# Sixteen chunks of the gate and up projections by seven half-size products where it were ten

## The chip, the cores and the metric

The kernel runs on one core of a Trainium2 chip. The metric is the device time of one execution in microseconds (us), the median of three runs. The engines are TensorE (PE, with its weight loads as PEld), VectorE (DVE), ScalarE (ACT), GpSimd (POOL) and SyncE (SP), which here only issues the loads of the weight stream.

## The reference

Two layers of a hybrid network on 512 tokens of width 1024 in float32. The change touches only the feed-forward part, which is computed twice with different weights (FFN1 and FFN2):

```
D_MODEL, SEQ, D_FF = 1024, 512, 2816

def _swiglu(x, w_gate, w_up, w_down):
    return (jax.nn.silu(x @ w_gate) * (x @ w_up)) @ w_down

h = _layer_norm(ALPHA * h + 0.5 * _swiglu(h, ffn1_w_gate, ffn1_w_up, ffn1_w_down), ln1_g, ln1_b)
...    # token mixers, cross attention
h = _layer_norm(ALPHA * h + 0.5 * _swiglu(h, ffn2_w_gate, ffn2_w_up, ffn2_w_down), ln4_g, ln4_b)
...    # second layer
```

## The kernel before

**Layout.** Activations stand feature by feature: `h[:, k]` holds features 128k to 128k+127 of all 512 tokens. Weights come from memory as a stream of strips of 128 x 1024 float32 (512 KB) into the four slots of `raw`. The 2816 hidden features are 22 chunks of 128; each chunk needs one strip of the gate weight and one of the up weight.

**Exact products.** Every float32 operand is split into a high part (`w_hi`, `a_hi`, `hid_hi`, made by ACT as a copy to the type float32r) and the rest (`w_lo`, `a_lo`, `hid_lo`, made by DVE as a subtraction). `product` (L422) issues three matmuls: high by high, high by low, low by high.

**Ordinary chunk.** `feature_strip` multiplies a strip with all 512 tokens: 8 blocks x 3 = 24 matmuls of 512 columns for gate, 24 for up. ACT takes the silu of the gate result (L1289), DVE multiplies it with the up result (L1321), ACT and DVE split the product into `hid_hi[:, c]` and `hid_lo[:, c]` (L1292, L1324).

**Fast chunk.** Gate and up strip together are a 2 x 2 block matrix (output: gate or up; input: first or second half of the features), and the activations are 2 x 2 as well (half of the features; half of the tokens). `pe_fast` multiplies them by a Strassen-Winograd scheme: seven products of half the features by half the tokens, each 4 blocks x 3 = 12 matmuls of 256 columns, so 84 in all. It needs four sums of weight quarters (S1 to S4), made per chunk by DVE in `raw` and `ctxv`, and four sums of activation quarters (T1 to T4), made once per feed-forward part: POOL subtracts into `ctxv` (L985), ACT and DVE split the sum (L991, L997). `t_raw`, `s21` and `flat21` are views of `ctxv`. The products of one fast chunk are issued in this order:

A11 (n), then S4 and A22 of chunk n-1, then S3, S2, A12 and S1 of chunk n; S3 meets T3, S2 meets T2, S1 meets T1, A22 meets T4.

**Order of a feed-forward part.** Chunks 0 to 3 are ordinary (the first four strips in an opening of their own), chunks 4 to 13 fast (`FAST_FROM`, `FAST = 4, 10`), chunks 14 to 21 ordinary, in a loop of two chunks a turn (`Fori`). After it comes the down projection. The four split token sums live in `hid_hi` and `hid_lo` at chunks 14 to 21 (`T_AT`), which are free until the first ordinary chunk behind the fast ones writes there.

**What sets the order.** Each engine has its own instruction list in program order, and semaphores stand between the lists: `f_hi`, `f_lo`, `f_mm`, `f_taken`, `f_joined`, `t_sum`, `f_sum` count the steps of the fast part, `strip_done` the strips that PE has finished, `proj_read` the banks of `proj` that have been read. A strip on PE waits for its `w_lo` and for its bank of `proj` (four banks, in turn). In `act_ffn` and `dve_ffn` the lists `ahead` say which splits stand ahead of the silu or of the gating of the first chunks.

Of the kernel before, what the change touches and what calls it, by code (L numbers as in the profile page):

```python
# [20 lines left out]
F32 = mybir.dt.float32  # L21
# [6 lines left out]
P = 128  # L28
# [56 lines left out]

FAST_FROM, FAST = 4, 10
G_FFN1 = 0
# [71 lines left out]
def hybrid_blocks(nc, stream, ada_in, cond_in, x_in, mem_in, ctx_in, cols_in, const_in, mask_in, rows_in, wst_in, band_in, rpb_in,  # L159
                  out):  # L160
    with ExitStack() as ctx:
# [3 lines left out]
        def sb(name, shape, dt=F32, scope=ctx):  # L165
            return scope.enter_context(nc.sbuf_tensor(name, shape, dt))
# [755 lines left out]
        A11, S3, A12, S2, S1, S4, A22 = range(7)  # L922
        T1, T2, T4, T3 = range(4)
        T_AT = FAST_FROM + FAST
        LAST_FAST = FAST - 1

        class Fast:


            def __init__(self, ffn, n):  # L930
# [29 lines left out]

        def token_sum(x, t):
            return x[:, T_AT + 2 * t:T_AT + 2 * t + 2].rearrange("p c t -> p (c t)")

# [9 lines left out]
        def pool_token_sums(pool, ffn):  # L973

            if ffn:
                pool.wait_ge(n_raw, LN3.r0 + KD)
                pool.wait_ge(ada_out, 1)
            else:
                for s in [in_xb] + in_x:
                    pool.wait_ge(s, 16)  # L980
            b11, b12, b21, b22 = (quarter(h, a, b) for a in range(2) for b in range(2))
            for t, x, y_ in ((T1, b12, b11), (T2, b22, t_raw), (T4, b21, t_raw), (T3, b12, b22)):
                if t:
                    pool.wait_ge(f_lo, (4 + 2 * FAST) * ffn + t)
                nc.gpsimd.tensor_tensor(t_raw, x, y_, ALU.subtract).then_inc(t_sum, 1)  # L985

        def act_token_sum(act, ffn, t):
            if ffn and t == 0:
                act.wait_ge(strip_done, S_FFN2)
            act.wait_ge(t_sum, 4 * ffn + t + 1)  # L990
            nc.scalar.activation(token_sum(hid_hi, t), flat21, ACT.Copy).then_inc(f_hi, 1)  # L991

        def dve_token_sum(dve, ffn, t):
            if ffn and t == 0:
                dve.wait_ge(strip_done, S_FFN2)
            dve.wait_ge(f_hi, (4 + 3 * FAST) * ffn + t + 1)
            nc.vector.tensor_tensor(token_sum(hid_lo, t), flat21, token_sum(hid_hi, t).bitcast(F32),  # L997
                                    ALU.subtract).then_inc(f_lo, 1)
# [76 lines left out]
        def tokens_of(t):  # L1075
            return [token_sum(x, t).rearrange("p (c t) -> p c t", t=HT) for x in (hid_hi, hid_lo)]

# [17 lines left out]
        def pe_fast(pe, f):  # L1095
# [71 lines left out]
        def act_fast(act, ffn):  # L1167
# [101 lines left out]

        def hid_chunk(x, i, n):  # L1270
            if isinstance(i, int):
                return x[:, 2 * i + n]
            return x[:, bass.ds(2 * i + FAST + n, 1)].rearrange("p a t -> p (a t)")

        def act_ffn(act, s0, g0):
# [3 lines left out]
            def two(i, done=0, ahead=None):  # L1279
                for j in range(4):  # L1280
                    st, g = Nth(s0 + done + j, 4, i), Nth(g0 + j, 4, i)
                    if ahead:
# [7 lines left out]
                    else:  # L1290
                        act.wait_ge(proj_read[g.slot], g.turn + 1)
                        nc.scalar.activation(hid_chunk(hid_hi, i, j // 2), work[:, j // 2], ACT.Copy).then_inc(hid_h, 1)  # L1292

            act_token_sum(act, ffn, T1)
            act_token_sum(act, ffn, T2)
            two(0, 0, [lambda: split_hi(act, Nth(s0 + 4)),
                       lambda: (split_hi(act, Nth(s0 + 5)), act_token_sum(act, ffn, T4)),
                       lambda: split_hi(act, Nth(s0 + 6)),
                       lambda: act_token_sum(act, ffn, T3)])
            two(1, 0, [lambda: split_hi(act, Nth(s0 + 7)), lambda: act_a11(act, fast), lambda: act_s3_a12(act, fast),  # L1300
                       lambda: act_s2_s1(act, fast)])
            act_fast(act, ffn)
            with act.Fori(2, (KF - FAST) // 2) as i:
                two(i, 2 * FAST)

        def dve_ffn(dve, s0, g0, hid0):
# [3 lines left out]
            def two(i, done=0, ahead=None):  # L1310
                for j in range(4):
                    st, g = Nth(s0 + done + j, 4, i), Nth(g0 + j, 4, i)
                    if ahead:
# [3 lines left out]
                    if j % 2:  # L1317
                        gate_g = Nth(g0 + j - 1, 4, i)
# [1773 lines left out]
```

## Time and profile before

| | before |
|---|---|
| time, median of 3 runs | 1695.29 us (1695.11 to 1695.45) |
| time of the profiled execution | 1695.29 us |
| its span (first to last instruction) | 1693.7 us |
| PE busy | 1673.8 us (99%) |
| DVE, ACT, POOL busy | 1103.4, 755.6, 187.1 us |
| granted TensorE clock | 1.0 |

The time of an execution is 1.6 us more than its span. An engine that is busy for 99% of the span is the one whose work and waits add up to the time; the other engines' idle time costs nothing as long as PE does not wait for them.

### The profile page before, as it was taken

The page shows a single profiled execution, that of the slowest core. Times are in us where ns is not written, and L with a number is a line of the kernel's source. Part 1 is how long each engine was busy: PE and PEld are TensorE (multiplying, and loading weights), DVE is VectorE, ACT ScalarE, POOL GpSimd, SP SyncE. Part 2 cuts the span into 40 slices and gives each one's busy share as a digit, 9 for nine tenths or more (in the row PEclk, how much of TensorE's full clock was granted, in tenths as well). Part 3 has the DMA queues.
Part 4 walks back from the last instruction along what each step waited for, and adds up shares of the span by engine and source line. Part 5 has one row for each costly group of instructions (what it writes and reads, how often), then busy time and mean ns, then how long its engine had stood idle before and what let it go on. Part 6 is the DMA issues. An engine that isn't in the chain of part 4 may idle for free.

```text
span 1693.7 us, 24497 instructions
## 1 busy us (share of the span) xinstructions
PE 1673.8 (99%) x9224; PEld 1413.3 (83%) x9224; DVE 1103.4 (65%) x1489; ACT 755.6 (45%) x1123; POOL 187.1 (11%) x166
## 2 busy tenths in 40 slices
PE   9999999999999999999999999999999999999999
PEld 7999888788787888887999888877878787788887
DVE  6886349987955784577886333457976968744442
ACT  5565222246455465434565222346555555733231
POOL 2000001012013521015000000022101020000000
PEclk9999999999999999999999999999999999999999
DMA  5334247633222353223334243323232222233331
GB/s 193 101 102 135 92 146 244 212 100 119 68 83 83 104 181 130 75 75 100 100 101 129 95 149 105 107 88 120 83 100 84 87 96 74 82 118 112 108 104 63
DMA packets 51497, 188.34 MB, mean 111 GB/s; under 512 B 5776, under 2 KB 6288, under 8 KB 50512
## 3 DMA queue, kind: packets, MB, share of 16 engines
q1 hardware_dynamic: 44640, 161.50, 29.2%
q10 hardware_dynamic: 5184, 16.00, 2.9%
q0 software_dynamic: 1584, 9.60, 1.6%
q8 instruction: 62, 1.02, 0.3%
q14 instruction: 27, 0.22, 0.0%
HBM read 182.89 MB, written 4.19 MB: 110 GB/s over the span
## 4 chain that ended last, share of the span: by engine, by line
PE 83%; DVE 9%; DMA 2%; ACT 2%; issue 2%; POOL 1%; SPq 0%; ACTq 0%; DVEq 0%; POOLq 0%
PE proj L427 68%; PE aux L427 8%; DVE w_lo L419 2%; DVE ada_prod L1455 1%; PE aux L2203 1%; PE aux L2190 1%; DMA ctxv<-ada_in 1%; DMA ctxk<-ada_in 1%; PE aux L1963 1%; PE aux L2180 1%; DMA raw<-stream 1%; ACT w_hi L412 0%; DVE score L1565 0%; DVE qk L1608 0%; POOL ctxv L985 0%
## 5 line engine op out<-in xcount | busy, mean ns | idle before, releaser
L419 DVE TENSOR_TENSOR w_lo<-raw,w_hi 128x1024 fp32r<-128x1024 f32 x260 | 332.3, 1280 | 299.5 <-ACT w_hi L412 293.4
L427 PE MATMUL proj<-a_hi,w_hi 128*128 128x512 f32 (+1 forms) x1216 | 476.7, 392 | 5.4 <-ACT sq L1289 2.2
L427 PE MATMUL proj<-a_hi,w_lo 128*128 128x512 f32 (+1 forms) x1216 | 466.9, 384 | 0.0
L427 PE MATMUL proj<-a_lo,w_hi 128*128 128x512 f32 (+1 forms) x1216 | 466.6, 384 | 0.0
L412 ACT ACTIVATE w_hi<-raw 128x1024 fp32r<-128x1024 f32 x254 | 267.1, 1054 | 224.0 <-PE proj L427 153.9
L427 PEld LDWEIGHTS proj<-a_hi,w_hi 128*128 128x128 f32 x1216 | 228.6, 188 | 58.1 <-issue 6.0
L427 PEld LDWEIGHTS proj<-a_lo,w_hi 128*128 128x128 f32 x1216 | 228.8, 188 | 45.9 <-issue 2.9
L427 PEld LDWEIGHTS proj<-a_hi,w_lo 128*128 128x128 f32 x1216 | 228.5, 188 | 45.8
L427 PE MATMUL proj<-hid_hi,w_hi 128*128 128x512 f32 (+1 forms) x534 | 187.6, 351 | 1.5 <-DVE w_lo L419 1.5
L427 PE MATMUL proj<-hid_hi,w_lo 128*128 128x512 f32 (+1 forms) x534 | 185.8, 348 | 0.0
L427 PE MATMUL proj<-hid_lo,w_hi 128*128 128x512 f32 (+1 forms) x534 | 185.8, 348 | 0.0
L427 PEld LDWEIGHTS proj<-hid_hi,w_hi 128*128 128x128 f32 x534 | 100.4, 188 | 15.9 <-DVE w_lo L419 2.4
L427 PEld LDWEIGHTS proj<-hid_hi,w_lo 128*128 128x128 f32 x534 | 101.1, 189 | 12.9
L427 PEld LDWEIGHTS proj<-hid_lo,w_hi 128*128 128x128 f32 x534 | 100.4, 188 | 13.5 <-issue 0.7
L2360 DVE SCALAR_TENSOR_TENSOR y<-glu,wtap,y 128x512 f32 (+1 forms) x120 | 90.5, 754 | 3.2
L427 PE MATMUL aux<-a_hi,w_hi 128*128 128x256 f32 x240 | 67.6, 282 | 1.1 <-ACT terms L1126 1.1
L427 PE MATMUL aux<-a_lo,w_hi 128*128 128x256 f32 x240 | 67.4, 281 | 0.0
L427 PE MATMUL aux<-a_hi,w_lo 128*128 128x256 f32 x240 | 67.4, 281 | 0.0
L1292 ACT ACTIVATE hid_hi<-work 128x512 f32 (+1 forms) x24 | 15.2, 632 | 98.1 <-DVE work L1321 98.1
L733 POOL TENSOR_SCALAR h<-h,cols 128x512 f32<-128x512 f32 x32 | 40.8, 1278 | 98.1 <-DVE a_lo L715 50.6
L1321 DVE TENSOR_TENSOR work<-sq,proj 128x512 f32<-128x512 f32 x24 | 16.4, 685 | 46.6 <-PE proj L427 46.6
L427 PEld LDWEIGHTS aux<-a_hi,w_hi 128*128 128x128 f32 x240 | 45.1, 188 | 1.5 <-issue 1.5
(409 smaller groups left out, 2753.1 us busy)
## 6 DMA issues: line engine op xcount, KB each, us to landing
raw<-stream SPq DMA_DIRECT2D x303, 512.0 KB, 3.7
ctxk<-ada_in ACTq DMA_DIRECT2D x12, 512.0 KB, 4.2
ctxv<-ada_in ACTq DMA_DIRECT2D x12, 512.0 KB, 4.2
out<-h ACTq DMA_DIRECT2D x7, 256.0 KB, 2.0
h<-x_in SPq DMA_DIRECT2D x3, 512.0 KB, 8.7
btab<-rpb_in POOLq DMA_DIRECT2D x4, 384.0 KB, 3.5
cond_row<-cond_in ACTq DMA_DIRECT2D x1, 1024.0 KB, 6.1
side<-mem_in POOLq DMA_DIRECT2D x1, 1024.0 KB, 5.2
```

Source lines behind the costliest of these rows:

```text
L412: nc.scalar.activation(w_hi[:, st.slot], raw[:, st.slot], ACT.Copy).then_inc(hi_ready, 1)
L419: nc.vector.tensor_tensor(w_lo[:, st.slot], raw[:, st.slot], w_hi[:, st.slot].bitcast(F32), ALU.subtract).then_inc(lo_ready, 1)
L427: mm = nc.tensor.matmul(dst, a, b, start=start and n == 0, stop=stop and n == 2, skip_group_check=onto)
L733: nc.gpsimd.tensor_scalar(m.dst[:, c], m.dst[:, c], 1.0, m.shift(c), ALU.mult, ALU.add).then_inc(n_raw, 1)
L1292: nc.scalar.activation(hid_chunk(hid_hi, i, j // 2), work[:, j // 2], ACT.Copy).then_inc(hid_h, 1)
L1321: nc.vector.tensor_tensor(work[:, j // 2], sq[:, j // 2], res, ALU.mult).then_inc(proj_read[g.slot], 1)
L1455: nc.vector.scalar_tensor_tensor(ada_prod[:, c], ada_w[t % 2], 1.0, cond_row[:, c], ALU.mult, ALU.mult, accum_out=modv[:, t, c:c + 1]).the ...
L1963: mm = nc.tensor.matmul(aux[:, u % 2, t * M:(t + 1) * M], xq[:, 2 * hd + kk, at:at + P], memk[:, 2 * hd + kk], start=(kk == 0), stop=(kk = ...
L2180: nc.tensor.matmul(aux[:, n, :M], nq[part, at], grid(nk[part], ROWS, BAND_AT[cb], BAND), start=True, stop=True)
L2190: mm = nc.tensor.transpose(aux[:, 2, b * P:(b + 1) * P], npr[:, u % 2, b * P:(b + 1) * P], ident)
L2203: mm = nc.tensor.matmul(aux[lo:lo + HD, 3, cb * P:(cb + 1) * P], v, npt[:, n, b * P:(b + 1) * P], start=(b == 0), stop=(b == 3))
L2360: ins = nc.vector.scalar_tensor_tensor(dst, src, wtap[:, tap:tap + 1], dst, ALU.mult, ALU.add)
```

## The change

Sixteen chunks (4 to 19) are fast instead of ten, in both feed-forward parts; chunks 20 and 21 stay ordinary, written out without a loop. The places 14 to 21 of `hid_hi` and `hid_lo` no longer hold all token sums: T3 and T2 go to a new tile `t_kept` (16 KB a partition), T4 to the last two chunks of `hid_hi` and `hid_lo`. T1 is no longer made by POOL: DVE subtracts it in two halves into `terms` and `work` (`dve_t1_sum`), ACT and DVE split it into the quarter of `a_hi` and `a_lo` (first half of the features, second half of the tokens) that no fast product reads (`act_t1`, `dve_t1`), once the eight ordinary strips are done; behind the last fast product that reads T1 the quarter is made again from `h` (`act_back`, `dve_back`), and the ordinary strip behind it takes the other half of the features first. T3 is now the first sum, T2 and T4 follow. Ahead of the first fast product stand one (FFN1) or two (FFN2) matmuls of constants (`pe_keep_clock`). The area for the descriptors of POOL's DMAs is cut from its default to 1024 bytes a partition.

```diff
-FAST_FROM, FAST = 4, 10
+FAST_FROM, FAST = 4, 16
...
+            t_kept = sb("t_kept", [P, 4, KD // 2 * HT], F32R, ph)
...
-        T1, T2, T4, T3 = range(4)
-        T_AT = FAST_FROM + FAST
+        T3, T2, T4, T1 = range(4)
+        SUMS, HIS, LOS = 3 * FAST + 2, 3 * FAST + 6, 2 * FAST + 6
...
-        def token_sum(x, t):
-            return x[:, T_AT + 2 * t:T_AT + 2 * t + 2].rearrange("p c t -> p (c t)")
+        def token_sum(t):
+            if t == T4:
+                return [x[:, KF - 2:].rearrange("p c t -> p (c t)") for x in (hid_hi, hid_lo)]
+            return [t_kept[:, 2 * t + n] for n in range(2)]
...
-            for t, x, y_ in ((T1, b12, b11), (T2, b22, t_raw), (T4, b21, t_raw), (T3, b12, b22)):
+            for t, x, y_ in ((T3, b12, b22), (T2, b11, t_raw), (T4, b21, t_raw)):
...
+        def t1_raw(n):
+            return (terms[:], work[:, 0].rearrange("p (a t) -> p a t", t=HT))[n]
+        def t1_part(x, n):
+            return x[:, 2 * n:2 * n + 2, HT:]
+        def dve_t1_sum(dve, ffn):
+            for n in range(2):
+                nc.vector.tensor_tensor(t1_raw(n), t1_part(h, n), h[:, 2 * n:2 * n + 2, :HT],
+                                        ALU.subtract).then_inc(f_sum, 1)
+        def act_t1(act, ffn):
+            act.wait_ge(strip_done, Fast(ffn, 0).end - 2)
+            for n in range(2):
+                act.wait_ge(f_sum, SUMS * ffn + 4 + n)
+                nc.scalar.activation(t1_part(a_hi, n), t1_raw(n), ACT.Copy).then_inc(f_hi, 1)
+        def dve_t1(dve, ffn):
+            for n in range(2):
+                dve.wait_ge(f_hi, HIS * ffn + 7 + n)
+                nc.vector.tensor_tensor(t1_part(a_lo, n), t1_raw(n), t1_part(a_hi, n).bitcast(F32),
+                                        ALU.subtract).then_inc(f_lo, 1)
+        def act_back(act, ffn):
+            act.wait_ge(f_mm, Fast(ffn, LAST_FAST).m5_done)
+            nc.scalar.activation(quarter(a_hi, 0, 1), quarter(h, 0, 1), ACT.Copy).then_inc(f_hi, 1)
+        def dve_back(dve, ffn):
+            dve.wait_ge(f_hi, HIS * (ffn + 1))
+            nc.vector.tensor_tensor(quarter(a_lo, 0, 1), quarter(h, 0, 1), quarter(a_hi, 0, 1).bitcast(F32),
...
             pe.wait_ge(f_taken, f.u1_seed)
+            if f.n == 0:
+                pe.wait_ge(f_lo, LOS * f.ffn + 7)
             fast_product(S1, tokens_of(T1), bank_p, onto=True).then_inc(f_mm, 1)
...
             nc.scalar.activation(bank_p, bank_u, ACT.Copy).then_inc(f_taken, 1)
+            if f.n == 0:
+                act.wait_ge(f_lo, LOS * f.ffn + 6)
             nc.scalar.activation(terms[:, 0], bank_u, ACT.Copy).then_inc(f_taken, 1)
...
             act_keep_v(act, f)
+            act_back(act, ffn)
             act_silu_two(act, f)
...
             dve_up_two(dve, f)
+            dve_back(dve, ffn)
             dve_up_one(dve, f)
...
-            pe.wait_ge(f_lo, (4 + 2 * FAST) * ffn + 4)
+            pe.wait_ge(f_lo, LOS * ffn + 3)
+            pe_keep_clock(1 + ffn)
             pe_mark_banks(pe, Fast(ffn, 0))
...
-            with pe.Fori(2, (KF - FAST) // 2) as i:
-                for j in range(4):
-                    if j == 1:
-                        pe.wait_ge(f_joined, last.up1)
-                    feature_strip(pe, Nth(s0 + 2 * FAST + j, 4, i), Nth(g0 + j, 4, i), a_hi, a_lo)
+            for j in range(4):
+                if j == 1:
+                    pe.wait_ge(f_joined, last.up1)
+                feature_strip(pe, Nth(last.end + j), Nth(g0 + 2 * FAST_FROM + j), a_hi, a_lo,
+                              order=(4, 5, 6, 7, 0, 1, 2, 3) if j == 0 else None,
+                              ready=lambda k: pe.wait_ge(f_lo, LOS * (ffn + 1)) if j == 0 and k == 0 else None)
...
-    nc = bacc.Bacc("TRN2", target_bir_lowering=False, num_devices=1)
+    nc = bacc.Bacc("TRN2", target_bir_lowering=False, num_devices=1, dynamic_dma_scratch_size=1024)
```

ACT at the start of FFN1, before: two token sums (`hid_hi<-ctxv`) stand ahead of the first strip's split (`w_hi<-raw`) and of the first silu (`sq<-proj`).

```order
15 L991 ACTIVATE hid_hi<-ctxv 128x1024 x2
16 L412 ACTIVATE w_hi<-raw 128x1024
17 L1289 ACT_TABLE_LOAD
18 L1289 ACTIVATE sq<-proj 128x512
19 L412 ACTIVATE w_hi<-raw 128x1024
20 L991 ACTIVATE hid_hi<-ctxv 128x1024
21 L1292 ACTIVATE hid_hi<-work 128x512
```

The same place now:

```order
15 L996 ACTIVATE t_kept<-ctxv 128x1024
16 L413 ACTIVATE w_hi<-raw 128x1024
17 L1334 ACT_TABLE_LOAD
18 L1334 ACTIVATE sq<-proj 128x512
19 L413 ACTIVATE w_hi<-raw 128x1024
20 L996 ACTIVATE t_kept<-ctxv 128x1024
21 L1337 ACTIVATE hid_hi<-work 128x512
```

One token sum, not two, stands ahead of the silu. The second stands where the third stood.

DVE where the ordinary strips end and the first fast chunk begins, before: the last weight split ahead (`w_lo<-ctxv`), the gating of chunk 3, then the steps of the second fast chunk.

```order
36 L1053 TENSOR_TENSOR w_lo<-ctxv,w_hi 128x1024
37 L1321 TENSOR_TENSOR work<-sq,proj 128x512
38 L1324 TENSOR_TENSOR hid_lo<-work,hid_hi 128x512
39 L1027 TENSOR_TENSOR w_lo<-raw,w_hi 128x512
40 L1004 TENSOR_TENSOR raw<-raw 128x512
41 L1064 TENSOR_TENSOR w_lo<-raw,w_hi 128x1024
```

The same place now:

```order
36 L1093 TENSOR_TENSOR w_lo<-ctxv,w_hi 128x1024
37 L1014 TENSOR_TENSOR terms<-h 128x512
38 L1014 TENSOR_TENSOR work<-h 128x512
39 L1366 TENSOR_TENSOR work<-sq,proj 128x512
40 L1369 TENSOR_TENSOR hid_lo<-work,hid_hi 128x512
41 L1027 TENSOR_TENSOR a_lo<-terms,a_hi 128x2x256
42 L1027 TENSOR_TENSOR a_lo<-work,a_hi 128x2x256
43 L1067 TENSOR_TENSOR w_lo<-raw,w_hi 128x512
44 L1044 TENSOR_TENSOR raw<-raw 128x512
45 L1104 TENSOR_TENSOR w_lo<-raw,w_hi 128x1024
```

Two sums of T1 stand ahead of the gating of chunk 3 and two splits of T1 behind it. ACT has its two copies of T1 ahead of the copy `hid_hi<-work` of chunk 3 for which the DVE row 40 waits.

PE at the same place, the last matmuls of the ordinary strips and the first of the fast chunk, before:

```order
192 L427 MATMUL proj<-a_lo,w_hi 128x512
193 L427 MATMUL proj<-a_hi,w_lo 128x512
194 L1085 MATMUL aux<-a_hi,w_hi 128x256 x2
195 L427 MATMUL aux<-a_hi,w_hi 128x256
196 L427 MATMUL aux<-a_lo,w_hi 128x256
```

and now:

```order
192 L428 MATMUL proj<-a_lo,w_hi 128x512
193 L428 MATMUL proj<-a_hi,w_lo 128x512
194 L546 MATMUL aux<-mean_d,ones_full 128x128
195 L1127 MATMUL aux<-a_hi,w_hi 128x256 x2
196 L428 MATMUL aux<-a_hi,w_hi 128x256
```

One float32 matmul of constants is new in FFN1, and two stand there in FFN2.

## Rows read from the trace of the kernel before

**Rows 1.** The page: span, engines, and granted clock by slice.

```profile
span 1693.7 us, 24497 instructions
PE 1673.8 (99%) x9224; PEld 1413.3 (83%) x9224; DVE 1103.4 (65%) x1489; ACT 755.6 (45%) x1123; POOL 187.1 (11%) x166
PEclk9999999999999999999999999999999999999999
```

**Rows 2.** Waits of PE by releaser: us in total, times, longest.

```profile
PE proj L427 <- ACT sq L1289: 2.2, 2, 1.6
...
PE aux L427 <- ACT terms L1126: 1.1, 2, 0.6
```

**Rows 3.** Timeline of PE, an ordinary strip: start, duration, instruction.

```profile
45.66 0.39 PE L427 MATMUL proj<-a_hi,w_lo 128*128 128x512 f32 x1
51.10 0.39 PE L427 MATMUL proj<-a_hi,w_lo 128*128 128x512 f32 x1
```

**Rows 4.** Chain of waits in FFN1's fast part: start, duration, engine and line.

```profile
61.61 2.83 PE proj L427 x24
...
140.76 2.83 PE proj L427 x24
```

**Rows 5.** Timeline of PE where it waits for the first silu, FFN1 and FFN2.

```profile
28.51 0.39 PE L427 MATMUL proj<-a_hi,w_lo 128*128 128x512 f32 x1
29.47 0.47 PE L427 MATMUL proj<-a_hi,w_hi 128*128 128x512 f32 x1 [0.58 <-ACT sq L1289]
...
790.74 0.39 PE L427 MATMUL proj<-a_hi,w_lo 128*128 128x512 f32 x1
792.75 0.47 PE L427 MATMUL proj<-a_hi,w_hi 128*128 128x512 f32 x1 [1.62 <-ACT sq L1289]
```

**Rows 6.** Timeline of ACT ahead of that silu, FFN1, then FFN2's two sums.

```profile
20.54 1.04 ACT L991 ACTIVATE hid_hi<-ctxv 128x1024 fp32r<-128x1024 f32 x1
25.41 1.06 ACT L991 ACTIVATE hid_hi<-ctxv 128x1024 fp32r<-128x1024 f32 x1 [3.83 <-POOL ctxv L985]
...
28.73 0.60 ACT L1289 ACTIVATE sq<-proj 128x512 f32<-128x512 f32 x1
...
783.76 1.06 ACT L991 ACTIVATE hid_hi<-ctxv 128x1024 fp32r<-128x1024 f32 x1 [4.81 <-POOL ctxv L985]
788.69 1.06 ACT L991 ACTIVATE hid_hi<-ctxv 128x1024 fp32r<-128x1024 f32 x1 [3.87 <-POOL ctxv L985]
```

**Rows 7.** Timeline of DVE from the last ordinary strip on.

```profile
48.47 1.22 DVE L1053 TENSOR_TENSOR w_lo<-ctxv,w_hi 128x1024 fp32r<-128x1024 f32 x1
51.52 0.69 DVE L1321 TENSOR_TENSOR work<-sq,proj 128x512 f32<-128x512 f32 x1 [1.84 <-PE proj L427]
52.91 0.69 DVE L1324 TENSOR_TENSOR hid_lo<-work,hid_hi 128x512 fp32r<-128x512 f32 x1 [0.70 <-ACT hid_hi L1292]
...
55.45 1.22 DVE L1064 TENSOR_TENSOR w_lo<-raw,w_hi 128x1024 fp32r<-128x1024 f32 x1
59.31 0.42 DVE L1143 TENSOR_TENSOR work<-proj,terms 128x256 f32<-128x256 f32 x1 [0.79 <-ACT terms L1126]
63.06 0.42 DVE L1148 TENSOR_TENSOR work<-proj,terms 128x256 f32<-128x256 f32 x1 [0.46 <-PE proj L427]
```

**Rows 8.** Timeline of ACT behind FFN1's last fast product but two.

```profile
147.86 0.38 ACT L1126 ACTIVATE terms<-aux 128x256 f32<-128x256 f32 x1
150.08 0.39 ACT L1134 ACTIVATE sq<-aux 128x256 f32<-128x256 f32 x1 [1.83 <-PE aux L427]
```

**Rows 9.** Float32 matmuls of constants: chain of waits, then PE's timeline.

```profile
753.52 0.86 PE aux L605 x2
...
1.75 4.64 PE L545 MATMUL aux<-mean_d,ones_full 128*128 128x128 f32 x20 [1.75 <-POOL eps_c L2562]
```

**Rows 10.** Busy time by window, fast stretch of FFN1, then of FFN2; PEclk is sixth.

```profile
61.60:140.80 79.20, 79.20 (x675) 79.20 (x674) 68.67 (x89) 49.97 (x88) 0.00 (x0) 1.00 0.33 107
824.90:904.00 79.10, 79.10 (x674) 79.10 (x673) 68.57 (x89) 49.96 (x87) 0.00 (x0) 1.00 0.33 107
```

More of the change, by code:

```diff
@@ L944, in __init__ @@
                 self.up2, self.up1, self.gated = range(3 * FAST * ffn + 3 * n + 1, 3 * FAST * ffn + 3 * n + 4)
-                self.s3, self.s21, self.s4 = range(3 * FAST * ffn + 3 * n + 1, 3 * FAST * ffn + 3 * n + 4)
-                hi = (4 + 3 * FAST) * ffn + 4 + 3 * n
+                t1 = 2 if n else 0
+                self.s3, self.s21, self.s4 = range(SUMS * ffn + 3 * n + t1 + 1, SUMS * ffn + 3 * n + t1 + 4)
+                hi = HIS * ffn + 3 + 3 * n + t1
                 self.hi11, self.hi_gate, self.hi21 = hi + 1, hi + 2, hi + 3
-                lo = (4 + 2 * FAST) * ffn + 4 + 2 * n
+                lo = LOS * ffn + 3 + 2 * n + t1
                 self.lo11, self.lo21 = lo + 1, lo + 2
@@ L981, in pool_token_sums @@
             b11, b12, b21, b22 = (quarter(h, a, b) for a in range(2) for b in range(2))
-            for t, x, y_ in ((T1, b12, b11), (T2, b22, t_raw), (T4, b21, t_raw), (T3, b12, b22)):
+            for t, x, y_ in ((T3, b12, b22), (T2, b11, t_raw), (T4, b21, t_raw)):
                 if t:
-                    pool.wait_ge(f_lo, (4 + 2 * FAST) * ffn + t)
+                    pool.wait_ge(f_lo, LOS * ffn + t)
                 nc.gpsimd.tensor_tensor(t_raw, x, y_, ALU.subtract).then_inc(t_sum, 1)
@@ L987, in act_token_sum @@
         def act_token_sum(act, ffn, t):
-            if ffn and t == 0:
+            if ffn and t == T3:
                 act.wait_ge(strip_done, S_FFN2)
-            act.wait_ge(t_sum, 4 * ffn + t + 1)
-            nc.scalar.activation(token_sum(hid_hi, t), flat21, ACT.Copy).then_inc(f_hi, 1)
+            act.wait_ge(t_sum, 3 * ffn + t + 1)
+            nc.scalar.activation(token_sum(t)[0], flat21, ACT.Copy).then_inc(f_hi, 1)
         def dve_token_sum(dve, ffn, t):
-            if ffn and t == 0:
+            if ffn and t == T3:
@@ L995, in dve_token_sum @@
                 dve.wait_ge(strip_done, S_FFN2)
-            dve.wait_ge(f_hi, (4 + 3 * FAST) * ffn + t + 1)
-            nc.vector.tensor_tensor(token_sum(hid_lo, t), flat21, token_sum(hid_hi, t).bitcast(F32),
+            dve.wait_ge(f_hi, HIS * ffn + t + 1)
+            hi, lo = token_sum(t)
+            nc.vector.tensor_tensor(lo, flat21, hi.bitcast(F32), ALU.subtract).then_inc(f_lo, 1)
+        def t1_raw(n):
+            return (terms[:], work[:, 0].rearrange("p (a t) -> p a t", t=HT))[n]
@@ L1075, in tokens_of @@
         def tokens_of(t):
-            return [token_sum(x, t).rearrange("p (c t) -> p c t", t=HT) for x in (hid_hi, hid_lo)]
+            if t == T1:
+                return part(0, 1)
+            return [x.rearrange("p (c t) -> p c t", t=HT) for x in token_sum(t)]
         def part(feature, token):
@@ L1280, in two @@
                 for j in range(4):
-                    st, g = Nth(s0 + done + j, 4, i), Nth(g0 + j, 4, i)
+                    st, g = Nth(s0 + 2 * done + 4 * i + j), Nth(g0 + 4 * i + j)
                     if ahead:
@@ L1291, in two @@
                         act.wait_ge(proj_read[g.slot], g.turn + 1)
-                        nc.scalar.activation(hid_chunk(hid_hi, i, j // 2), work[:, j // 2], ACT.Copy).then_inc(hid_h, 1)
-            act_token_sum(act, ffn, T1)
-            act_token_sum(act, ffn, T2)
+                        nc.scalar.activation(hid_hi[:, done + 2 * i + j // 2], work[:, j // 2],
+                                             ACT.Copy).then_inc(hid_h, 1)
+            act_token_sum(act, ffn, T3)
             two(0, 0, [lambda: split_hi(act, Nth(s0 + 4)),
-                       lambda: (split_hi(act, Nth(s0 + 5)), act_token_sum(act, ffn, T4)),
+                       lambda: (split_hi(act, Nth(s0 + 5)), act_token_sum(act, ffn, T2)),
                        lambda: split_hi(act, Nth(s0 + 6)),
-                       lambda: act_token_sum(act, ffn, T3)])
+                       lambda: act_token_sum(act, ffn, T4)])
             two(1, 0, [lambda: split_hi(act, Nth(s0 + 7)), lambda: act_a11(act, fast), lambda: act_s3_a12(act, fast),
-                       lambda: act_s2_s1(act, fast)])
+                       lambda: (act_s2_s1(act, fast), act_t1(act, ffn))])
             act_fast(act, ffn)
-            with act.Fori(2, (KF - FAST) // 2) as i:
-                two(i, 2 * FAST)
+            two(2, FAST)
         def dve_ffn(dve, s0, g0, hid0):
@@ L1311, in two @@
                 for j in range(4):
-                    st, g = Nth(s0 + done + j, 4, i), Nth(g0 + j, 4, i)
+                    st, g = Nth(s0 + 2 * done + 4 * i + j), Nth(g0 + 4 * i + j)
                     if ahead:
@@ L1317, in two @@
                     if j % 2:
-                        gate_g = Nth(g0 + j - 1, 4, i)
+                        gate_g = Nth(g0 + 4 * i + j - 1)
+                        c = done + 2 * i + j // 2
                         res = result(dve, st, g)
@@ L1322, in two @@
                                                 ALU.mult).then_inc(proj_read[g.slot], 1)
-                        dve.wait_ge(hid_h, hid0 + done // 2 + j // 2 + 1 + 2 * i)
-                        nc.vector.tensor_tensor(hid_chunk(hid_lo, i, j // 2), work[:, j // 2],
-                                                hid_chunk(hid_hi, i, j // 2).bitcast(F32),
+                        dve.wait_ge(hid_h, hid0 + c + 1)
+                        nc.vector.tensor_tensor(hid_lo[:, c], work[:, j // 2], hid_hi[:, c].bitcast(F32),
                                                 ALU.subtract).then_inc(hid_l, 1)
-            dve_token_sum(dve, ffn, T1)
-            dve_token_sum(dve, ffn, T2)
+            dve_token_sum(dve, ffn, T3)
             two(0, 0, [lambda: split_lo(dve, Nth(s0 + 4)),
-                       lambda: (split_lo(dve, Nth(s0 + 5)), dve_token_sum(dve, ffn, T4)),
+                       lambda: (split_lo(dve, Nth(s0 + 5)), dve_token_sum(dve, ffn, T2)),
                        lambda: split_lo(dve, Nth(s0 + 6)),
-                       lambda: dve_token_sum(dve, ffn, T3)])
+                       lambda: dve_token_sum(dve, ffn, T4)])
             two(1, 0, [lambda: split_lo(dve, Nth(s0 + 7)),
@@ L1336, in dve_ffn @@
                        lambda: (dve_s2_s1(dve, fast), dve_s4(dve, fast), dve_s3_a12(dve, fast)),
-                       lambda: dve_lo_s2_s1(dve, fast)])
+                       lambda: (dve_lo_s2_s1(dve, fast), dve_t1_sum(dve, ffn))])
+            dve_t1(dve, ffn)
             dve_fast(dve, ffn)
-            with dve.Fori(2, (KF - FAST) // 2) as i:
-                two(i, 2 * FAST)
+            two(2, FAST)
         DOWN_SQUARES = {16: (0, 1), 17: (2, 3), 18: (4,), 19: (5,), 22: (6,)}
```

4 lines of the change are left out of this document (removed).

## The prediction

> **What bounds the kernel now.** I read the page first: TensorE is busy for 99% of a span of 1693.7 us, at a granted clock of 9 tenths or more in every slice [rows 1]. So time comes from two things only, PE's work and PE's waits. The waits of PE by releaser come next; two of the named ones touch the feed-forward parts: 2.2 us in two waits for the silu of L1289, and 1.1 us in two waits for the ACT copy at L1126 [rows 2]. Then the timelines, for what PE's work costs there. One ordinary strip is 24 matmuls of 512 columns, and 24 starts after 45.66 us PE is at 51.10 [rows 3]: 5.44 us, or 0.227 us a matmul, and 10.88 us for the gate and the up strip of a chunk. (The 0.39 us that a row gives as duration overlaps with its neighbours; only starts may be counted.) In the fast part the chain of waits has one stretch of 24 matmuls into `proj` (A22 and S3) per chunk; the first such stretch behind chunk 4 starts at 61.61 and the eighth after it at 140.76 [rows 4]. That is 79.15 us for eight chunks, 9.894 a chunk, or 0.1178 us for each of its 84 matmuls. PE is busy through that whole stretch [rows 10], so this is its own pace, not that of another engine.
>
> **The change part by part.**
>
> *Six more fast chunks in each part.* Each trades 10.88 us for 9.894, which gives 0.986 us; twelve give **11.8 us**. The starts are printed to 0.01 us, which leaves 0.2 on the sum. The pace could be lower only if DVE or ACT could not follow for sixteen chunks as they do for ten. In the window of eight chunks DVE is busy for 68.67 us of 79.20 and ACT for 49.97, so DVE has 1.3 us to spare a chunk, and what it splits for a chunk depends on nothing older than the chunk before. A queue that holds for ten chunks holds for sixteen. The stream needs a strip per 4.95 us instead of 5.44 for 60 us more, and moves 107 GB/s in the fast window with PE never idle [rows 10].
>
> The Trainium skill, page "TensorE: Matmul & The Clock Gate", section "Back-to-back issue gap", speaks against the change: in a stream of weight loads and matmuls it gives about 81 ns at 128 columns and 131 ns at 512, and a point between them for 256 columns, about 98 ns as an estimate, would make a fast chunk 8.2 us against 6.3 for an ordinary one. By it the twelve chunks would cost 23 us. The starts above show 117.8 and 226.6 ns, so the trace does not agree, and its numbers are used.
>
> *One token sum ahead of the silu, not two.* PE starts a strip late at 29.47, 0.96 us behind the start before it, and at 792.75, 2.01 us behind [rows 5]; less 0.23 for the matmul itself that is 0.73 and 1.78. The reason stands in ACT's timeline: the second sum's copy comes only at 25.41 and at 788.69, since POOL can subtract T2 only when DVE has read T1, and the split and the silu of the first strip stand behind it in ACT's list [rows 6]. In the new order only the first sum, done at 21.6 and 784.8, is ahead. Now the strip itself is the limit. In FFN1's opening the last 18 matmuls belong to the third and fourth strip, so the first two are done by 28.74 - 18 x 0.227 = 24.7. In FFN2's, the last 27 do, which gives 790.97 - 6.1 = 784.8. From the end of a sum's copy to the silu's start are 2.3 us (26.47 to 28.73), the silu takes 0.6: its bank is free at about 27.8 and 787.8, before PE asks for it at 28.74 and 790.97. Both waits go: **2.5 us**. The second sum now stands behind the second strip's split, with 5.4 us of the next strip ahead of its first user, so nothing new is late there; T4 keeps its place.
>
> *T1 at the start of the fast part.* Six instructions per part. The two subtractions fall into DVE's idle 1.84 us ahead of 51.52 [rows 7], 2 x 0.6 us behind the split that ends at 49.7. At about 51.5 the eighth strip is done and ACT copies twice. The halves have 512 elements a partition, as L1324 with 0.69 us, and follow each other at about 0.6. So ACT is busy to 52.7, and only then copies chunk 3's `hid_hi`, to 53.3; before, DVE's L1324 began at 52.91. Now it starts about 53.3, the two splits of T1 follow, and T1 is whole at 55.2. PE needs it for the fifth product, S1: 51.32 + 0.24 for the marks + four products of 1.41 = 57.2. It comes 2 us early. Behind the splits DVE is late with the next chunk: L1027 at 55.1 instead of 54.11, L1064 at 56.4 instead of 55.45, L1143 at 59.4 instead of 59.31, where it had waited for 0.79 us [rows 7]. The wait at 63.06 takes up the rest. PE wants L1064's result about 60.0 (one chunk of five products and A11), so nothing reaches PE: **0**.
>
> *T1's quarter made again.* ACT's copy of 1024 elements (1.04 us [rows 6]) goes between L1126, which ends at 148.24, and L1134, which starts at 150.08 after 1.83 us of waiting [rows 8]. It is hidden. DVE's subtraction of 1.22 us follows and is done about 150.6; the strip begins about 151.4 and asks for the quarter only after four blocks, 2.7 us later. **0**. The 0.6 us waits for L1126 stay.
>
> *Constant matmuls.* One in FFN1, two in FFN2. PE does not wait there before, so they add. A float32 matmul of constants with 512 columns takes 0.86 us in the chain, a quarter of it is 0.215; at the kernel's start ten of 128 columns took 4.64 us, 0.464 each [rows 9]. I take the first, since PE has long been busy here: **0.65 us lost**; bounds are 0 (if they only fill a wait) and 1.4.
>
> *Loop written out, one POOL subtraction less, smaller descriptor area.* PE shows no wait at the turns of the loop, and POOL is busy for 11%. The area has no row. POOL's DMAs are few, and a queue that holds fewer of them could only delay the second of two; neither of PE's waits shown [rows 2] is for POOL's loads. I take 0, bounds 0 and 3 us.
>
> Sum: 11.8 + 2.5 - 0.65 = 13.7. The profiled execution took 1695.29 us, which is also the median, so the forecast is **1681.6 us**, 0.8% faster. What a measurement of this kernel can tell from no change is about 0.2%, 3.4 us.
>
> **The rivals.**
>
> *T1 is late (14%).* For it speaks that three engines pass it on in 4 us, and DVE is the busiest engine after PE. If the copies and the splits took what 1024 elements take (1.05 and 1.22 us), T1 would be whole 2.2 us later, which uses up the margin of 2 us, and DVE would come 2.2 us later to the next chunk. PE would wait 0.2 to 2.5 us in each part: 1682 to 1686.5 us. Against it: half the elements, half the time in every row.
>
> *The wait for the silu stays (5%).* If something else than the second sum held up ACT, 2.5 us are not won: 1684.1 us. Against it, ACT's row at 25.41 names POOL as releaser.
>
> *Slower by the clock (2%).* The unbroken stretch of half-size products goes from 99 to 158 us, each part. If the granted clock fell from its upper level (2.4 GHz) to the lower (1.2 GHz) in it, a chunk would take 19.8 us instead of 9.9. The change gives 13.7 us, so it takes 1.4 chunks at the low level to lose it all and 1.7 to be slower than the bound: with four such chunks the time would be 1721 us. Against it: 1.00 granted in both fast windows, with weight loads back to back in them [rows 10].
>
> *Half-size products lose (1%)*, by 23 us to 1705 us as the issue-gap rule named above would have it, and twenty chunks before show otherwise.
>
> *The change does nothing that can be measured (2%).* A wait of 5 us or more in each part, as of POOL's loads in a short queue, would bring 1691.9 to 1698.7 us.
>
> *More is won (4%).* A wait behind the feed-forward part, such as the one for the ACT copy (1.1 us), could shrink: 1679.5 us.
>
> The forecast itself has the other 72%.
>
> **How the numbers follow.** The forecast's own spread is 0.2 for the pace, 0.7 for the constants and 0.5 for pieces of waits left over: 1680.5 to 1682.8. To reach 8 in 10 and more, the range takes in the late T1 and the silu's wait: 1680.0 to 1686.0. Faster: 0.72 + 0.14 + 0.05 + 0.04 = 0.95. Same 0.02, slower 0.03.
>
> **What would show it right or wrong.** The stretches of 24 matmuls into `proj` in the chain should stand 9.89 us apart, fifteen of them in each part. The two waits for the silu of L1289 (now L1334) should be gone. Between the last ordinary strip and the first fast product a gap of 0.2 us in FFN1 and 0.4 in FFN2 should be seen. PE should not wait for `a_lo` at the fifth product, and the DVE row behind T1 (L1189 now) should start within 0.2 us of where it did, counted from the end of the strips. The prediction is wrong if PE waits for DVE in the first two fast chunks, if a chunk takes over 9.95 us, or if the granted clock is below 1 in the fast part.

## The result, and the profile after

The changed kernel takes **1674.48 us** (median of 4 runs, 1674.17 to 1674.93), against 1695.2 for the kernel before on the same chip: a ratio of 0.9878 [0.9866, 0.9889], 20.7 us faster. I had forecast 1681.6 with a range of 1680.0 to 1686.0. The sign is right, but the gain is 7 us above the 13.7 of the sum, and it lies outside the range.

The page of the kernel after, in the lines that answer [rows 1]:

```profile
span 1673.3 us, 25423 instructions
PE 1655.3 (99%) x9662; PEld 1417.7 (85%) x9662; DVE 1165.1 (70%) x1581; ACT 795.0 (48%) x1211; POOL 182.6 (11%) x164
PEclk9999999999999999999999999999999999999999
```

PE is still busy for 99%, now in 438 more instructions, at an unchanged granted clock. So the time still is PE's work and PE's waits. The waits of PE by releaser, in the columns of [rows 2], the top rows and the one of the feed-forward part:

```profile
PE aux L2016 <- DVE xp L2058: 2.1, 3, 0.9
PE proj L428 <- DVE a_lo L915: 1.8, 3, 0.9
PE aux L546 <- POOL eps_c L2605: 1.7, 1, 1.7
PE proj L428 <- DVE w_lo L420: 1.7, 3, 0.7
...
PE aux L428 <- ACT terms L1172: 1.1, 2, 0.6
...
PE proj L428 <- DVE a_lo L2802: 0.7, 1, 0.7
```

The 2.2 us for the silu are gone from the list, and the 1.1 us for the ACT copy (L1126 before, L1172 now) stand as they did. One row is new, 0.7 us for `a_lo` in the kernel's opening, ahead of the feed-forward part; the same wait is 0.2 us in k00, and 0.4 and 0.7 us in bscr and b12, two edits of the kernel before. Among the waits in the feed-forward parts' fast chunks none has come. ACT's timeline shows how, first in FFN1, then in FFN2:

```profile
20.61 1.04 ACT L996 ACTIVATE t_kept<-ctxv 128x1024 fp32r<-128x1024 f32 x1
...
26.55 0.60 ACT L1334 ACTIVATE sq<-proj 128x512 f32<-128x512 f32 x1
...
776.93 1.06 ACT L996 ACTIVATE t_kept<-ctxv 128x1024 fp32r<-128x1024 f32 x1 [4.81 <-POOL ctxv L990]
780.25 0.60 ACT L1334 ACTIVATE sq<-proj 128x512 f32<-128x512 f32 x1
```

One sum stands ahead of the silu, which now ends at 27.15 us; before it only started at 28.73 [rows 6], as PE was about to ask for its bank.

What I had not forecast stands in the chain of waits. FFN1's fast part first (start, duration, engine and line), then FFN2's:

```profile
50.60 0.22 PE aux L546 x2
50.82 0.24 PE aux L1127 x2
...
60.95 2.83 PE proj L428 x24
63.78 7.07 PE aux L428 x60
...
199.46 2.83 PE proj L428 x24
...
806.07 0.44 PE aux L546 x4
806.52 0.24 PE aux L1127 x2
...
816.28 2.72 PE proj L428 x24
819.00 6.80 PE aux L428 x60
...
949.56 2.72 PE proj L428 x24
```

From the first to the last of those stretches of 24 are fourteen chunks in each part. In FFN1 they take 199.46 - 60.95 = 138.51 us, 9.894 a chunk, exactly as in [rows 4]. In FFN2 the same instructions take 949.56 - 816.28 = 133.28 us, **9.520 a chunk**, and every piece is 4% shorter (2.72 for 2.83, 6.80 for 7.07). The busy times of both stretches, in the columns of [rows 10]:

```profile
60.95:199.46 138.51, 138.51 (x1179) 138.51 (x1178) 120.24 (x155) 87.83 (x153) 0.00 (x0) 1.00 0.33 107
816.28:949.56 133.28, 133.28 (x1178) 133.28 (x1178) 120.07 (x155) 87.89 (x153) 0.00 (x0) 1.00 0.34 112
```

PE is never idle in either, the granted clock is 1.00 (the upper level, 2.4 GHz) in both, and DVE and ACT do the same work. So it isn't another engine and it isn't the clock: PE's own stream has two paces. Grouped by line and form, 61 to 140 us, weight loads and matmuls of FFN1 (count, then busy us and mean ns of one):

```profile
L428 PE MATMUL aux<-a_lo,w_hi 128*128 128x256 f32 x128 | 36.0, 281 | 0.0
...
L428 PEld LDWEIGHTS aux<-a_hi,w_hi 128*128 128x128 f32 x128 | 24.6, 192 | 0.0
L428 PEld LDWEIGHTS aux<-a_lo,w_hi 128*128 128x128 f32 x128 | 24.0, 188 | 0.0
L428 PEld LDWEIGHTS aux<-a_hi,w_lo 128*128 128x128 f32 x128 | 24.0, 188 | 0.0
```

and the same view of 817 to 896 us in FFN2:

```profile
L428 PE MATMUL aux<-a_lo,w_hi 128*128 128x256 f32 x128 | 35.3, 276 | 0.0
...
L428 PEld LDWEIGHTS aux<-a_hi,w_hi 128*128 128x128 f32 x128 | 24.0, 188 | 0.0
```

In the slow stream a matmul's row says 281 ns and every third weight load 192; in the quick one 276 and 188 for all. (The load that takes 192 ns is that of the first matmul of each three here; in the kernel before it is that of the second.) The starts give the pace: 9.894 us / 84 = 117.8 ns from one matmul to the next in FFN1, 9.520 us / 84 = 113.3 ns in FFN2. The 16 chunks of FFN2 save 16 x (9.894 - 9.520) = **6.0 us**. That is nearly all of the missing 7.

What differs between the parts right ahead of the stream is the count of constant matmuls: one in FFN1, two in FFN2. It could also be the place in the program, FFN2's transfers, or the one layout of instructions that happened to come out. That is what the experiments are for.

### The profile page after: what moved, and what is told of

It is laid out like the page before. It is cut to its first block, busy times and chain, and to the rows that moved or that the text cites. A ratio compares the mean times of both kernels' runs of the same rounds, so it can differ in the third digit from the quotient of the medians.

```text
span 1673.3 us, 25423 instructions
## 1 busy us (share of the span) xinstructions
PE 1655.3 (99%) x9662; PEld 1417.7 (85%) x9662; DVE 1165.1 (70%) x1581; ACT 795.0 (48%) x1211; POOL 182.6 (11%) x164
## 4 chain that ended last, share of the span: by engine, by line
PE 85%; DVE 8%; DMA 2%; issue 2%; ACT 2%; POOL 0%; SPq 0%; DVEq 0%; ACTq 0%; POOLq 0%
PE proj L428 65%; PE aux L428 13%; DVE w_lo L420 2%; DVE ada_prod L1498 1%; PE aux L2246 1%; PE aux L2233 1%; DMA ctxv<-ada_in 1%; DMA ctxk<-ada_in 1%; PE aux L2006 1%; PE aux L2223 1%; DVE score L1608 0%; DVE qk L1651 0%; DVE md L1629 0%; PE aux L2226 0%; PE aux L572 0%
## 5 line engine op out<-in xcount | busy, mean ns | idle before, releaser
L428 PE MATMUL proj<-a_hi,w_hi 128*128 128x512 f32 (+1 forms) x1024 | 401.7, 392 | 3.9 <-DVE a_lo L915 1.8
L428 PE MATMUL proj<-a_hi,w_lo 128*128 128x512 f32 (+1 forms) x1024 | 392.1, 383 | 0.0
L428 PE MATMUL proj<-a_lo,w_hi 128*128 128x512 f32 (+1 forms) x1024 | 391.8, 383 | 0.0
L428 PEld LDWEIGHTS proj<-a_lo,w_hi 128*128 128x128 f32 x1024 | 192.6, 188 | 38.6 <-issue 2.9
L428 PE MATMUL aux<-a_hi,w_hi 128*128 128x256 f32 x512 | 142.7, 279 | 1.1 <-ACT terms L1172 1.1
L428 PE MATMUL aux<-a_lo,w_hi 128*128 128x256 f32 x512 | 142.6, 278 | 0.0
L428 PE MATMUL aux<-a_hi,w_lo 128*128 128x256 f32 x512 | 142.6, 278 | 0.0
L428 PEld LDWEIGHTS aux<-a_hi,w_hi 128*128 128x128 f32 x512 | 97.2, 190 | 1.5 <-issue 1.5
L428 PEld LDWEIGHTS aux<-a_lo,w_hi 128*128 128x128 f32 x512 | 96.1, 188 | 0.0
L428 PEld LDWEIGHTS aux<-a_hi,w_lo 128*128 128x128 f32 x512 | 96.1, 188 | 0.0
```

The lines of the kernel that those rows point to most:

```text
L428: mm = nc.tensor.matmul(dst, a, b, start=start and n == 0, stop=stop and n == 2, skip_group_check=onto)
```

## The experiments

Every time is the median of its runs; the ratio is to the kernel before, run on the same chip; "pace" is the start-to-start time of the 256-column matmuls in the fast part of FFN1 / FFN2, from the trace. b12 and bscr are edits of the kernel before, all others are edits of the changed one. The runs were made on several chips, each with the kernel before beside it, so between chips the ratios say more than the times.

| kernel | constants FFN1, FFN2 | us | ratio | pace, ns |
|---|---|---|---|---|
| before | 0, 0 | 1695.2 | | 117.8 / 117.8 |
| after | 1, 2 | 1674.48 | 0.9878 [0.9866, 0.9889] | 117.8 / 113.3 |
| k00 | 0, 0 | 1680.04 | 0.9908 [0.9892, 0.9925] | 117.8 / 117.8 |
| k21 | 2, 1 | 1673.75 | 0.9872 [0.9856, 0.9889] | 113.3 / 117.8 |
| k34 | 3, 4 | 1674.08 | 0.9877 [0.9861, 0.9894] | 117.8 / 113.3 |
| k65 | 6, 5 | 1674.84 | 0.9886 [0.9872, 0.9900] | 113.3 / 117.8 |
| k22 | 2, 2 | 1668.06 | 0.9843 [0.9829, 0.9856] | 113.3 / 113.3 |
| m34 | 0, 0; 3, 4 marks | 1678.87 | 0.9907 [0.9892, 0.9922] | 117.8 / 117.8 |
| b12 (before) | 1, 2 | 1691.58 | 0.9979 [0.9970, 0.9989] | 117.8 / 113.3 |
| bscr (before) | 0, 0; small area | 1694.72 | 0.9998 [0.9988, 1.0007] | 117.8 / 117.8 |
| a10n | 0, 0; ten chunks | 1691.10 | 0.9978 [0.9969, 0.9987] | 117.8 / 117.8 |
| kh | 2, 2 and two more places | 1668.33 | 0.9847 [0.9834, 0.9859] | 113.3 / 113.3 |
| k22b | 2, 2 again | 1668.39 | 0.9845 [0.9833, 0.9858] | 113.3 / 113.3 |

### Is it the constant matmuls, and where?

**k00** takes them out.

```diff
             pe.wait_ge(f_lo, LOS * ffn + 3)
-            pe_keep_clock(1 + ffn)
             pe_mark_banks(pe, Fast(ffn, 0))
```

> The changed kernel without its constant matmuls ahead of the fast parts. Theory A (the pace of a stream of 256-column matmuls is one of two, 117.8 or 113.3 ns, settled at its start by what PE does just before it): FFN2's chunks go back from 9.52 to 9.89 us, 16 x 0.374 = 6.0 us lost, 0.65 us of constants saved, so about 1679.8 us. Theory B (FFN2's stream is faster because of the new layout or place of the program, and the constants only cost their time): FFN2's chunks stay at 9.52 us, time about 1673.8 us.

Measured: 1680.04 us (1678.41 to 1680.72), 5.6 us slower than after (6.3 slower than k21, its neighbour on the same chip), where 6.0 - 0.65 = 5.3 were expected of the constants. The chain of waits of k00 in FFN2:

```profile
805.95 0.24 PE aux L1127 x2
...
816.08 2.83 PE proj L428 x24
```

Without the constants FFN2 goes at the pace of before. This kernel is also my forecast's sum without its constants term: 1695.0 - 11.8 - 2.5 = 1680.7, measured 1680.04.

**k21** turns the counts round: two in FFN1, one in FFN2.

```diff
-            pe_keep_clock(1 + ffn)
+            pe_keep_clock(2 - ffn)
```

> The changed kernel with two constant matmuls in FFN1 and one in FFN2 (it has one and two). Theory A, if the count alone settles the pace: the paces change places, 9.52 us a chunk in FFN1 and 9.89 in FFN2, time the same, about 1674.5 us. Theory A, if count and place both matter: any of both paces in each part, 1668.5, 1674.5 or 1680.5 us. Theory B: paces stay, 1674.5 us.

The fast pace changed parts. The chain of k21, FFN1 and FFN2:

```profile
50.77 0.44 PE aux L546 x4
...
51.46 1.36 PE aux L428 x12
...
799.75 0.22 PE aux L546 x2
...
800.21 1.41 PE aux L428 x12
```

Twelve matmuls take 1.36 us behind two constants and 1.41 behind one, wherever these stand. FFN2's place and its transfers are ruled out. The time, 1673.75 us, is that of after within its interval.

**b12** puts the same line into the kernel before and changes nothing else. There too it stands ahead of the two marks, short float32r matmuls of 128 by 256 with which each fast part opens its two banks (L1085 before, L1127 now).

```diff
             pe.wait_ge(f_lo, (4 + 2 * FAST) * ffn + 4)
+            pe_keep_clock(1 + ffn)
             pe_mark_banks(pe, Fast(ffn, 0))
```

> The kernel before (ten fast chunks) with one constant matmul ahead of FFN1's fast part and two ahead of FFN2's, and nothing else. Theory A: FFN2's ten chunks go from 9.89 to 9.52 us, 3.7 us gained, 0.65 lost, about 1692.2 us. Theory B: both parts stay at 9.89 us, about 1695.9 us.

Measured: 1691.58 us (10 runs), 3.4 us less than 1695.01 beside it. FFN2 has ten fast chunks there: 10 x 0.374 - 0.65 = 3.1 expected. The chain of b12, with 2.72 behind two constants once more:

```profile
814.17 0.45 PE aux L545 x4
...
824.38 2.72 PE proj L427 x24
```

So the rest of the change isn't needed for it, and after, k21 and b12, with different layouts of instructions, show it alike: a lucky placement of the program is unlikely.

### Is it "at least two", or the engine's recent work?

**k34** gives three and four, **k65** six and five, **k22** two and two.

```diff
-            pe_keep_clock(1 + ffn)
+            pe_keep_clock(3 + ffn)
```

> The changed kernel with three constant matmuls in FFN1 and four in FFN2. Theory A, if an even count gives the fast pace: FFN1 9.89 and FFN2 9.52 us, about 1675.4 us; if it is not the parity, the paces move. Theory B: paces stay, 0.9 us more for four matmuls, 1675.4 us.

```diff
-            pe_keep_clock(1 + ffn)
+            pe_keep_clock(6 - ffn)
```

> The changed kernel with six constant matmuls in FFN1 and five in FFN2. So far counts of 2 and 4 gave 113.3 ns a matmul, 0, 1 and 3 gave 117.8. If parity settles it (theory A-even): FFN1 at 9.52 us a chunk, FFN2 at 9.89, and 11 constants at about 0.11 to 0.22 us each, so about 1674.5 + 0.9 to 1.8 us. If any count from 4 up will do (theory A-enough): both at 9.52, about 1669 to 1670 us.

Three in FFN1 leave 117.8, four in FFN2 give 113.3; six in FFN1 give 113.3, five in FFN2 leave 117.8. The chain of k34 in FFN1, then that of k65 in FFN1 and FFN2:

```profile
50.31 0.67 PE aux L546 x6
...
51.21 1.41 PE aux L428 x12
```

```profile
50.38 1.34 PE aux L546 x12
...
51.97 1.36 PE aux L428 x12
...
799.25 1.11 PE aux L546 x10
...
800.60 1.41 PE aux L428 x12
```

So it is not "enough of them": 2, 4 and 6 give the quick pace, 0, 1, 3 and 5 don't. (Each constant is two rows, 0.22 us.) Both kernels end within their intervals of after, though k65 pays 8 more constants, 1.8 us.

```diff
-            pe_keep_clock(1 + ffn)
+            pe_keep_clock(2)
```

> The changed kernel with two constant matmuls ahead of both fast parts. Theory A (the number of constant matmuls just ahead settles the pace, and two give the fast one whatever the part): both parts at 9.52 us a chunk, 6.0 us gained over the changed kernel less 0.2 for one matmul more, about 1668.5 us. Theory C (only one of the two parts can have the fast pace, since k21 gave it to FFN1 and took it from FFN2): 1674.7 us.

Measured: **1668.06 us** (1667.36 to 1669.41), 27.1 us below the kernel before and 6.4 below after (5.9 by the two ratios, whose intervals don't meet); 6.0 - 0.22 = 5.8 were expected. It beats both kernels. In the windows of k22, both parts over fourteen chunks:

```profile
61.10:194.38 133.28, 133.28 (x1179) 133.28 (x1178) 120.26 (x155) 87.87 (x153) 0.00 (x0) 1.00 0.34 112
809.46:942.74 133.28, 133.28 (x1178) 133.28 (x1178) 120.11 (x155) 87.87 (x153) 0.00 (x0) 1.00 0.34 112
```

The two parts are equal to the hundredth. Run again as **k22b**, it took 1668.39.

> k22 again beside kh on the same chip: about 1668.1 us, both fast parts at 113.3 ns a matmul.

**m34** asks whether extra float32r matmuls do it. It has no constants, but three of the marks in FFN1 and four in FFN2, instead of two.

```diff
-            for bank in (bank_p, bank_u):
+            for bank in (bank_p, bank_u, bank_p, bank_u)[:3 + f.ffn]:
...
-            pe_keep_clock(1 + ffn)
```

> The changed kernel without constant matmuls; the two marking matmuls of 256 columns (float32r) ahead of the first fast chunk become three in FFN1 and four in FFN2. Theory A1 (the count of short matmuls ahead settles the pace, whatever their kind): one of the two parts at 9.52 us a chunk, about 1674.3 us. Theory A2 (the float32 constants, other than float32r matmuls, shift the weight loads): both parts stay at 9.89, about 1680.3 us.

Both parts stay at 117.8 and the time, 1678.87 us, is that of k00 within the intervals. But the marks aren't without effect. The load of 192 ns is that of `a_hi,w_lo` in both parts of k00 and of the kernel before; in m34 it moves, in FFN1 (one mark more, 61 to 140 us), then in FFN2 (two more, 817 to 896 us):

```profile
L428 PEld LDWEIGHTS aux<-a_lo,w_hi 128*128 128x128 f32 x128 | 24.6, 192 | 0.0
...
L428 PEld LDWEIGHTS aux<-a_hi,w_hi 128*128 128x128 f32 x128 | 24.6, 192 | 0.0
```

Two marks more, which are two rows, leave it where one constant, also two rows, leaves it in FFN1 of after. So m34 shows that one and two more marks don't give the quick pace. It doesn't show that it takes float32: the match of two constants would be four more marks, and that wasn't run.

**kh** asks whether two constants also help the other streams of 256 columns that run at 119.9 ns: the half strips of the down projection and the memory keys.

```diff
+            pe_keep_clock(2)
             half(0, 0)
...
             for n in range(lo, hi):
+                if n == 1:
+                    pe_keep_clock(2)
```

> Two constant matmuls ahead of both fast parts as in k22, and two more ahead of two other streams of 256 columns: the half strips at the end of FFN1's down projection (about 130 matmuls at 119.9 ns) and the second strip of the memory's keys (about 170 at 119.9 ns). If two constants give any such stream the pace of 113.3 ns: 300 x 6.6 ns = 2.0 us gained, 0.9 lost, about 1667.0 us. If the other streams' pace has another reason: 0.9 us lost, about 1669 us.

They don't. The time is that of k22b beside it. Behind their two constants the half strips' matmuls start 119.9 ns apart, as in the kernel before, and the memory keys' keep their 283 ns (by line and form, 570 to 612 us of kh):

```profile
L428 PE MATMUL proj<-side_lo,w_hi 128*128 128x256 f32 x64 | 18.1, 283 | 0.0
```

### The other parts of the change

**a10n** is the changed order with ten fast chunks and no constants: what the new order of the token sums is worth by itself. The ordinary strips that are left are written out behind the fast part as before.

```diff
-FAST_FROM, FAST = 4, 16
+FAST_FROM, FAST = 4, 10
...
-            for j in range(4):
+            for j in range(2 * (KF - FAST - FAST_FROM)):
...
-            two(2, FAST)
+            for i in range(2, (KF - FAST) // 2):
+                two(i, FAST)
```

> Ten fast chunks as before, everything else as in the changed kernel (T1 made by DVE in a quarter of a_hi and a_lo, T3 first, quarter made again, no loop), and no constant matmuls. The prediction's sum for the order of the token sums and for T1: 2.5 us gained, 0 lost, 1692.5 us. Rival (handing on T1 costs a wait of PE in the first fast chunks): 1693 to 1697 us.

Measured: 1691.10 us; by the ratio a gain of 3.7 us over before (2.2 to 5.3), where 2.5 were forecast for the two waits. They are gone from its list, and none for T1 has come. Two other waits differ too: PE waits 2.0 us for `w_lo` before and 1.1 in a10n, and 0.4 us for `a_lo` in the opening of a10n, where the kernel before has none. From here to k00, the twelve further fast chunks alone, the ratios give 11.9 us, with an uncertainty of 3, where I had 11.8; the pace is 117.8 ns in both.

**bscr** is the kernel before with the small descriptor area.

```diff
-    nc = bacc.Bacc("TRN2", target_bir_lowering=False, num_devices=1)
+    nc = bacc.Bacc("TRN2", target_bir_lowering=False, num_devices=1, dynamic_dma_scratch_size=1024)
```

> The kernel before with the area for POOL's DMA descriptors cut to 1024 bytes a partition, which also moves every tile down by 15 KB. Prediction: nothing, 1695.0 us and both paces at 117.8 ns. Rival (the area or the tiles' places count): a change of over 1 us, or another pace of the 256-column streams.

Measured: 1694.72 us, 0.9998 [0.9988, 1.0007]. It costs nothing that can be measured.

## Why the prediction was off

**Six more fast chunks: right where the pace was that of before, mis-sized in FFN2.** I took 9.894 us a chunk for all thirty-two. FFN1's sixteen go at it to the last digit. FFN2's go at 9.520, and that takes not only the six new chunks but also the ten old ones: 16 x 0.374 = 6.0 us. DVE and ACT kept pace for sixteen chunks, as forecast.

**Constant matmuls: the step that failed.** Their price as work was right: 0.22 and 0.44 us in the chain after, against 0.65 forecast for the three. But I priced them as time alone, with bounds of 0 and 1.4 us lost, and no gain among the bounds. What they do to the stream behind them is worth nine times their price. k00 (they are gone, and with them 5.6 us), k21 (they change places, and so does the pace) and b12 (they alone give 3.4 us to the kernel before) show that the term had to be +5.3, not -0.65.

The evidence was in the trace of the kernel before, in rows that I didn't look at. By line and form, all of its span:

```profile
L427 PE MATMUL proj<-ctx_lo,w_hi 128*128 128x256 f32 x32 | 8.8, 276 | 0.0
...
L427 PE MATMUL aux<-a_lo,w_hi 128*128 128x256 f32 x240 | 67.4, 281 | 0.0
```

These are two streams of the same form of matmul at two speeds. Their starts are 113.6 and 117.8 ns apart, and the quicker one comes right behind four float32 matmuls that multiply data by a constant matrix (L605 to L613, two rows each; the first of them stands in [rows 9]). From [rows 4] I had read one pace and called it PE's own. Had I compared the streams of one form, the list of rivals would have had a case "the constants change the pace", up to 16 x 0.374 = 6.0 us a part. In which part it would come, no row of before tells.

**Token sum ahead of the silu: right.** Both waits are gone, as the list shows. ACT's silu started at 26.55 and 780.25, in time. Worth 2.5 by the rows; a10n's 2.2 to 5.3 holds it, with 0.5 us from other waits in it.

**T1 at the start of the fast part: right.** DVE's timeline behind the last ordinary strip, to be read against [rows 7]:

```profile
52.34 0.69 DVE L1369 TENSOR_TENSOR hid_lo<-work,hid_hi 128x512 fp32r<-128x512 f32 x1 [1.02 <-ACT hid_hi L1337]
52.95 0.68 DVE L1027 TENSOR_TENSOR a_lo<-terms,a_hi 128x512 fp32r<-128x512 f32 x1
53.55 0.69 DVE L1027 TENSOR_TENSOR a_lo<-work,a_hi 128x512 fp32r<-128x512 f32 x1
...
58.65 0.42 DVE L1189 TENSOR_TENSOR work<-proj,terms 128x256 f32<-128x256 f32 x1
```

T1 is whole at 54.24. PE starts the fifth product four products of 1.41 us behind 51.06, at 56.7: 2.5 us to spare, 2 forecast. L1189 starts 8.05 us behind the end of the strips (50.60), where it was 7.83 (51.48 to 59.31): 0.2 late, which is the time of the constant matmul in between, and PE doesn't wait for it. The rival "T1 is late" is out.

**T1's quarter made again: right.** ACT's copy runs in the idle time ahead of the next copy, with 0.85 us of it left:

```profile
206.84 1.05 ACT L1033 ACTIVATE a_hi<-h 128x1024 fp32r<-128x1024 f32 x1
208.74 0.38 ACT L1180 ACTIVATE sq<-aux 128x256 f32<-128x256 f32 x1 [0.85 <-PE aux L428]
```

**Descriptor area and loop: right**, 0 by bscr and by the waits.

**Rivals.** None of those with a price came. "More is won" named the right side with the wrong mechanism (a wait that shrinks) and 2.1 of the 7.1 us. "Half-size products lose" is out: FFN1's stream kept 117.8 ns over sixteen chunks.

The sum with the term put right: 11.8 + 2.5 - 0.65 + 6.0 = 19.7 for 20.7 measured. The last 1.0 is within the uncertainty of the ratio (0.0012, 2 us); PE's waits for `w_lo`, 2.0 us before and 1.7 after, vary from kernel to kernel (1.5 in k00, 0.5 in k22) with no edit at their place, and so does the one in the opening. The rest of the 1.0 isn't traced to a cause.

## What to carry to other kernels

When PE is busy for all of a stretch, its pace is still a number to be compared: list the streams of one form of matmul over the whole kernel, and if two of them differ by a few ns at the same granted clock, find out what stands ahead of each. An added instruction has a price as work and can change the pace of what stands behind it; its range needs a bound on the side of a gain too, as large as the difference between those streams. And a change that "keeps something alive" is best tried with counts of 0, 1, 2 and 3 in each place: here one more constant in FFN1 was worth another 6 us.

## What the runs showed of the hardware

- In these kernels, streams of float32r matmuls with 256 columns and a weight load each have three paces at a granted clock of 1.00: 113.3 ns (row of 276 ns, all loads 188), 117.8 (281; every third load 192), and 119.9 (283; nearly all loads 192). Strips of 512 columns keep 226.7 ns, which is 2 x 113.3. The loads mark the pace but don't make up the difference: three matmuls differ by 13 ns, the one load by 4.
- The pace holds from the first product up to PE's wait for L1172, ahead of a part's last two products. That restart can change it: behind it FFN1's last matmuls start 114.1 ns apart in after, and 117.8 in the kernel before. They are quick there in every part that has a constant, odd counts too, and in FFN2 of m34; they stay at 117.8 in before, bscr, a10n, k00 and FFN1 of m34.
- In this place the pace depends on the float32 constant matmuls just ahead: 2, 4 or 6 gave 113.3 ns in every one of the eight kernels that have such a count, in either part; 0, 1, 3 or 5 gave 117.8 in all others.
- The slow streams aren't all in one state. The load of 192 ns is the second of each three behind two marks alone, the third behind three marks, and the first behind four marks as well as behind two marks with 1, 3 or 5 constants. So two more marks and one constant, each two rows, leave PE in the same state by every sign that the traces have: pace, place of the load, and the quick restart.
- Why is open. Counted in extra rows from two on, the results repeat with every four (2, 6 and 10 slow, 4, 8 and 12 quick), but zero, which would have to be quick, is slow, and two constants don't help the streams at 119.9 (kh). No run separates the kind of data from the number of rows or from the time that they take (0.22 us for a constant, 0.24 for two marks). Four more marks instead of two constants would; so would a pair of float32 matmuls of another shape, or of half the columns. None of these was tried.
